# Cross-attention with its loop written out: three PSUM sets, one bank for the sample's heads, outputs written as two parts

## What is computed

```python
def memory_cross_attention(h, mem_k, mem_v, w_q, w_o):     # XA_HEADS = 4, XA_HEAD_DIM = 256, N_MEM = 256
    q = (h @ w_q).reshape(B, L, XA_HEADS, XA_HEAD_DIM)
    s = jnp.einsum('blhd,bmhd->bhlm', q, mem_k).astype(jnp.float32) * (XA_HEAD_DIM ** -0.5)
    p = jax.nn.softmax(s, axis=-1).astype(mem_v.dtype)
    o = jnp.einsum('bhlm,bmhd->blhd', p, mem_v)
    return o.reshape(B, L, D_MODEL) @ w_o
```

## Time and profile before

| | |
|---|---|
| median of 3 runs | 2229.95 us (2228.45 to 2230.43) |
| profiled execution | 2233.87 us, of which the span from the first to the last instruction is 2232.2 us |
| PE busy | 2114.9 us (95%) |
| DVE busy | 1206.9 us (54%) |
| ACT busy | 529.2 us (24%) |
| POOL busy | 189.9 us (9%) |
| mean granted TensorE clock | 0.970 |

### The profile page before, as it was taken

One profiled execution on the slowest core, in us unless ns is written; L12 is line 12 of the kernel. 1 busy time (PEld: TensorE's weight loads), 2 busy tenths in 40 slices (PEclk: granted clock), 3 DMA queues, 4 the chain that ended last, 5 costly groups with the idle time before them and its releaser, 6 DMA issues. The chain is left out here.

```text
span 2232.2 us, 49063 instructions
## 1 busy us (share of the span) xinstructions
PE 2114.9 (95%) x21806; PEld 2009.3 (90%) x21806; DVE 1206.9 (54%) x1695; ACT 529.2 (24%) x971; POOL 189.9 (9%) x255
## 2 busy tenths in 40 slices
PE   8998989998999999996999899998999899999997
PEld 8996769985999999994979899987997799999997
DVE  5435777444655555338549444445663565555433
ACT  2005774013211110002247222225221221101000
POOL 4000001000200000110000322210011010000010
PEclk9998999998999999998999999998999999999998
DMA  4334112460233223231311000004341123222221
GB/s 127 90 111 125 58 29 86 128 184 0 79 88 88 85 85 90 86 89 45 90 57 39 8 4 4 4 13 125 114 161 48 31 85 92 85 85 85 86 86 66
DMA packets 299347, 169.81 MB, mean 76 GB/s; under 512 B 10312, under 2 KB 294160, under 8 KB 299184
## 3 DMA queue, kind: packets, MB, share of 16 engines
q1 hardware_dynamic: 294960, 151.25, 23.5%
q10 hardware_dynamic: 4224, 16.12, 1.9%
HBM read 155.94 MB, written 11.41 MB: 75 GB/s over the span
## 5 line engine op out<-in xcount | busy, mean ns | idle before, releaser
L259 PE MATMUL psum<-words_r,weights_high_r 128*128 128x272 f32 (+1 forms) x7808 | 1498.7, 291 | 16.9 <-DVE words_r L210 13.2
L259 PEld LDWEIGHTS psum<-words_r,weights_high_r 128*128 128x128 f32 x7808 | 1235.9, 190 | 27.2 <-issue 15.0
L259 PE MATMUL psum<-words_r,weight_ring_r 128*128 128x272 f32 (+1 forms) x3904 | 1131.8, 290 | 0.0
L259 PEld LDWEIGHTS psum<-words_r,weight_ring_r 128*128 128x128 f32 x3904 | 739.5, 189 | 0.0
L205 DVE TENSOR_SCALAR weights_high_r<-weight_ring 128x1024 fp32r<-128x1024 f32 (+1 forms) x258 | 176.3, 683 | 522.8 <-PE psum L259 515.3
L210 DVE TENSOR_TENSOR weight_ring_r<-weight_ring,weights_high_r 128x1024 fp32r<-128x1024 f32 (+1 forms) x264 | 319.3, 1209 | 11.2 <-ACT weights_high_r L344 2.4
L399 POOL TENSOR_TENSOR words<-words,words 128x544 f32<-128x544 f32 x42 | 74.5, 1773 | 1283.0 <-ACT words L386 1283.0
L2370 PE MATMUL psum<-words 64*64 64x64 f32 (+1 forms) x3536 | 138.6, 231 | 0.6
L1707 ACT ACTIVATE words<-words 128x544 f32<-128x544 f32 x44 | 29.0, 659 | 454.7 <-DVE words L1650 454.7
L2370 PEld LDWEIGHTS psum<-words 64*64 64x64 f32 x3536 | 129.1, 135 | 3.1 <-DVE words L2293 1.8
L376 DVE TENSOR_TENSOR words<-psum,words 128x544 f32<-128x544 f32 x48 | 34.8, 724 | 129.3 <-PE psum L259 129.3
(11 more groups left out here) (309 smaller groups left out, 1960.2 us busy)
## 6 DMA issues: line engine op xcount, KB each, us to landing
weight_ring<-in_ffn_w_gate_up_dram SPq DMA_DIRECT2D x88, 512.0 KB, 3.8
weight_ring<-in_xa_w_kv_dram SPq DMA_DIRECT2D x32, 512.0 KB, 3.9
weight_ring<-in_ffn_w_down_dram SPq DMA_DIRECT2D x32, 448.0 KB, 3.7
weight_ring<-in_sb_w_qkv_dram SPq DMA_DIRECT2D x24, 512.0 KB, 3.7
weight_ring<-in_xa_w_q_dram SPq DMA_DIRECT2D x16, 512.0 KB, 4.1
weight_ring<-in_xa_w_o_dram SPq DMA_DIRECT2D x16, 512.0 KB, 4.0
weight_ring<-in_ffn_w_down_dram SPq DMA_DIRECT2D x16, 512.0 KB, 4.0
weight_ring<-in_sb_w_o_dram SPq DMA_DIRECT2D x8, 512.0 KB, 4.0
```

What stands on the lines that cost most here:

```text
L259: last = nc.tensor.matmul(c.psum[0:job.m(u), job.bank(q) + h, 0:w], weights[:, k, :], x[:, k, h * w:(h + 1) * w], start=job.opens(u) and k ...
```

## The change

`cross_attention` is written out for four heads, without a loop, copies to fixed buffers or primed semaphores, and POOL has nothing left to do in it. Head g uses PSUM set g % 3 (two banks), so three heads can be open at a time; the fourth waits until the outputs of the first are taken (`o_low`). Banks 6 and 7 belong to the sample. Its four heads lie together in one bank, each in 32 partitions (`lanes`), so that one maximum, one exponential and one scaling serve all; its values are multiplied the other way round (the probabilities are the stationary operand), and the result is transposed back. Maxima are taken over two query tiles at a time. The outputs leave PSUM as halves: ACT writes the high part of a tile, DVE subtracts it and writes the low part; `full` is not written. The order of work on each engine is a written list. In `feed_forward` the `Split` of the attention's outputs is gone, and the column sum of the norm (`norm.tensor`) moves from between units 0 and 1 of `up` into unit 1, after its second tile. The stage makes 23 semaphores instead of 38, the following one 2 fewer. The scratch space changes with it. The ring's weight splits are as before.

```diff
--- before.py
+++ after.py
@@ cross_attention
...
-            with pool.Fori(0, XH // 2) as it:
-                for g, hd in enumerate(heads):
-                    pool.wait_ge(s("scored_s", g), it + PRIMED)
-                    nc.gpsimd.tensor_copy(hd.q, q[:, bass.ds(it * 4 + 2 * g, 2), :]).then_inc(s("q_staged", g), 1)
...
+            def score(g):
+
+                if g >= SETS:
+                    pe.wait_ge(o_low, 2 * (g - SETS) + 2)
+                for i in range(QT):
+                    for kk in range(2):
+                        last = mm(scores(g)[:, i, :], q[:, 2 * g + kk, i * P:(i + 1) * P], kv[:, 2 * g + kk, :],
+                                  start=kk == 0 and i % 2 == 0, stop=kk == 1, skip_group_check=True)
+                    if i % 2:
+                        last.then_inc(scored, 1)
...
+            def score_sample():
+
+                for kk in range(2):
+                    for g, r in enumerate(lanes):
+                        last = mm(c.psum[r, 6, 0:NMEM], q[:, 2 * g + kk, SEQ:T], s_kt[:, 2 * g + kk, :], start=kk == 0, stop=kk == 1,
+                                  skip_group_check=True)
+                last.then_inc(scored_s, 1)
...
+            def weigh(g):
+
+                pe.wait_ge(first_copied, g + 1)
+                pe.wait_ge(second_copied, g + 1)
+                for e in range(2):
                     for m in range(MT):
-                        for i in range(QT):
-                            last = nc.tensor.transpose(hd.wide[m][:, i * P:(i + 1) * P], hd.prob[:, i, m * P:(m + 1) * P], c.ident[:])
...
+                        last = mm(bank(g, e), kv_rows[:, m, D + (2 * g + e) * P:D + (2 * g + e + 1) * P], prob_t[g % SETS][:, m, :],
+                                  start=m == 0, stop=m == MT - 1)
+                    last.then_inc(weighed, 1)
+
+            def weigh_sample():
+
+                pe.wait_ge(copied_s, 1)
+                for m in range(MT):
+                    for g, r in enumerate(lanes):
+                        last = mm(c.psum[r, 7, 0:NMEM], prob_ts[:, m, r], s_v[:, m, 2 * g * P:2 * (g + 1) * P], start=m == 0, stop=m == MT - 1,
+                                  skip_group_check=True)
+                last.then_inc(weighed_s, 1)
...
+            score(0)
+            score(1)
+            score_sample()
+            score(2)
+            turn(0)
+            turn(1)
+            weigh(0)
+            turn_sample()
+            weigh(1)
+            score(3)
+            turn(2)
+            weigh_sample()
+            weigh(2)
+            turn_out_sample()
+            turn(3)
+            weigh(3)
...
+            def take_out(g, e):
+
+                dve.wait_ge(o_high, 2 * g + e + 1)
+                take_low(c, o.low[:, 2 * g + e, 0:SEQ], bank(g, e), o.high[:, 2 * g + e, 0:SEQ]).then_inc(o_low, 1)
+
+            peak(0, 0)
+            peak(0, 1)
+            peak(1, 0)
+            peak(1, 1)
+            scale(0)
+            peak_sample()
+            peak(2, 0)
+            scale(1)
+            peak(2, 1)
+            copy_first(0)
+            copy_first(1)
+            scale_sample()
+            scale(2)
+            take_out(0, 0)
+            take_out(0, 1)
+            take_out(1, 0)
+            take_out(1, 1)
+            peak(3, 0)
+            peak(3, 1)
+            copy_first(2)
+            dve.wait_ge(weighed_s, 1)
+            nc.vector.tensor_copy(rows_s, c.psum[:, 7, 0:NMEM]).then_inc(rows_s_copied, 1)
+            scale(3)
+            take_out(2, 0)
+            take_out(2, 1)
+            for e in range(2):
+                dve.wait_ge(o_s_high, 2)
+                take_low(c, sample_tiles(o.low, e), sample_out(e), sample_tiles(o.high, e)).then_inc(o_s_low, 1)
+            copy_first(3)
+            take_out(3, 0)
+            take_out(3, 1)
...
+            def take_out(g):
+
+                for e in range(2):
+                    act.wait_ge(weighed, 2 * g + e + 1)
+                    nc.scalar.activation(o.high[:, 2 * g + e, 0:SEQ], bank(g, e), ACT.Copy).then_inc(o_high, 1)
+
+            exp(0)
+            exp(1)
+            exp_sample()
+            copy_second(0)
+            copy_second(1)
+            exp(2)
+            take_out(0)
...
+            take_out(1)
+            exp(3)
+            copy_second(2)
+            take_out(2)
...
+            copy_second(3)
+            take_out(3)
@@ feed_forward
+            def sum_norm(k):
+
+                if k == 1:
+                    pe.wait_ge(c.slot_emptied[3], up.emptied[3])
+                    norm.tensor(pe)
+
             for u in range(o.per):
-                multiply_unit(c, pe, o, 0, u, split.low if u == 0 else None)
-            multiply_unit(c, pe, up, 0, 0, norm.low)
-            pe.wait_ge(c.slot_emptied[3], up.emptied[3])
-            norm.tensor(pe)
-            for u in range(1, RING):
+                multiply_unit(c, pe, o, 0, u)
+            for u in range(RING):
                 if u == 3:
                     pe.wait_ge(norm.meaned, 1)
-                multiply_unit(c, pe, up, 0, u)
+                multiply_unit(c, pe, up, 0, u, norm.low if u == 0 else None, sum_norm if u == 1 else None)
...
-            split.scalar(act)
...
             split_unit(c, dve, o, 0, 0)
-            split.vector(dve)
             split_unit(c, dve, o, 0, 1)
```

More of the change, by code:

```diff
@@ L1518, in cross_attention @@
-    heads = [Head(g) for g in range(2)]
-    assert at[0] <= 3 * REGION
-    def s(x, g):
-        return heads[g].sems[x]
+        for w in spaces:
+            if w[2] >= n:
+                ap = c.flat(w[0], n, at=w[1])
+                w[1] += n
+                w[2] -= n
+                return ap if len(shape) == 1 else ap.rearrange("p (a b) -> p a b", a=shape[0])
+        raise AssertionError("no space")
+    prob, prob_t = [part(QT, NMEM) for _ in range(SETS)], [part(MT, SEQ) for _ in range(SETS)]
@@ new lines, in cross_attention @@
+    neg_max, total, inverse = (part(XH, QT) for _ in range(3))
+    prob_s, prob_ts, rows_s = part(NMEM), part(MT, P), part(NMEM)
+    stats_s = part(3)
+    neg_max_s, total_s, inverse_s = (stats_s[:, i:i + 1] for i in range(3))
+    lanes = [slice(g * DEC, (g + 1) * DEC) for g in range(XH)]
+    scored, maxed, exped, inverted, scaled, turned, first_copied, second_copied, weighed, o_high, o_low = (c.sem(f"{name}_{x}") for x in (
+        "scored", "maxed", "exped", "inverted", "scaled", "turned", "first_copied", "second_copied", "weighed", "o_high", "o_low"))
@@ new lines, in score_sample, with turn @@
+            def score_sample():
[4 more added lines that the diff above has]
+                last.then_inc(scored_s, 1)
+            def turn(g):
+                pe.wait_ge(scaled, QT * (g + 1))
+                for m in range(MT):
+                    for i in range(QT):
+                        last = tr(bank(g, m)[:, i * P:(i + 1) * P], prob[g % SETS][:, i, m * P:(m + 1) * P], c.ident[:])
+                    last.then_inc(turned, 1)
@@ L1632, in feed_forward, with exp, exp_sample @@
-def feed_forward(c, name, o, up, down, nxt, split, norm, tail, hidden, gated, out):
+            def exp(g):
+                for i in range(QT):
+                    act.wait_ge(maxed, 2 * g + i // 2 + 1)
+                    nc.scalar.activation(prob[g % SETS][:, i, :], scores(g)[:, i, :], ACT.Exp, bias=neg_max[:, g, i:i + 1],
+                                         accum_out=total[:, g, i:i + 1]).then_inc(exped, 1)
+            def exp_sample():
+                act.wait_ge(maxed_s, 1)
+                nc.scalar.activation(prob_s, c.psum[:, 6, 0:NMEM], ACT.Exp, bias=neg_max_s, accum_out=total_s).then_inc(exped_s, 1)
@@ new lines, in copy_second @@
+            def copy_second(g):
+                act.wait_ge(turned, MT * g + 2)
+                nc.scalar.copy(prob_t[g % SETS][:, 1, :], bank(g, 1)).then_inc(second_copied, 1)
+            def take_out(g):
+                for e in range(2):
+                    act.wait_ge(weighed, 2 * g + e + 1)
[4 more added lines that the diff above has]
+            copy_second(0)
@@ new lines, in _ @@
+            copy_second(1)
+            exp(2)
+            take_out(0)
+            act.wait_ge(turned_s, 1)
+            nc.scalar.copy(prob_ts, c.psum[:, 6, 0:NMEM].rearrange("p (m t) -> p m t", m=MT)).then_inc(copied_s, 1)
+            take_out(1)
+            exp(3)
+            copy_second(2)
+            take_out(2)
+            act.wait_ge(o_s_turned, 1)
+            for e in range(2):
+                nc.scalar.activation(sample_tiles(o.high, e), sample_out(e), ACT.Copy).then_inc(o_s_high, 1)
@@ L1638, in feed_forward @@
+            copy_second(3)
+            take_out(3)
+def feed_forward(c, name, o, up, down, nxt, norm, tail, hidden, gated, out):
     nc = c.nc
```

155 lines of the change are left out of this document (47 added, 108 removed).

## The result

The changed kernel takes 2200.45 us (median of 4 runs, 2196.48 to 2203.73), the kernel before 2230.19 (4 runs). The ratio is 0.9863, with a 95% interval of 0.9842 to 0.9884. That is 29.7 us less by the medians, where 27.1 were forecast (2203). The profiled execution has a span of 2198.3 us.

What follows compares the result with a forecast made beforehand. PE, busy 95% of the span, was taken as the bound. Stages of 44.55 us against 59.96 and 42.05 against 54.99, with 1.16 returning later, gave 27.1 us less: 2203 us, forecast 2199 to 2207, range 2194 to 2214.

Steps and rivals of the forecast that it cites:

- What bounds the stage: Whole kernel: PE is busy 95% of the span, so time is saved where it works slowly or stands still.
- PE's products: Attention stage, higher clock: 33.0 us for four heads, 0.5 small transposes, 2.2 sample, 1.8 waits; 37.5 us in all.
- The sample's products: Sample's scores and weighing: four column groups share the array, 1.1 us each, bounds 0.9 and 3.63; serial rival chance 0.1.
- The change of shape: At the sample's two products: switching to narrow column groups costs about 0.2 us, included in the 1.1 each.
- The waits: PE inside the stage: 0.4 us before weigh(2), 1.4 before weigh(3), all other waits met.
- Entrance and end: PE starts about 0.5 us after the last work before; last product to first of the projection takes 1.5 + 2.55.
- The clock: Layer 0's entrance: a low stretch loses 2.5 us, bounds 0 and 3.3; layer 1's entrance stays at the higher level.
- a fall there: Rival, inside the stage at turn(0), turn(1) and the sample's narrow products: clock falls, up to 3.3 us a layer; chance 0.15.
- the low stretch there stays in both layers, at the same cost: Start of the projection: PE stands still 4.05 us, between 3.5 and 4.7 before, so no difference in clock loss.
- The semaphores: Clearing behind layer 1's attention: the same 1.16 us is paid one stage later, before the outputs are stored; net nothing.
- The size of the whole: Both stretches: 15.4 us less in layer 0, 12.9 in layer 1, 1.16 returning later; together 27.1.
- The halves: Outputs as halves: 1.5 us after the last product, formerly hidden; the next stage's first low part, 0.6 us, goes.

Runs made afterwards that it cites:

- written-out kernel before: The kernel before with its two-pass loop written out and POOL's copies gone, all else as before: 2233.86 us, ratio 1.0003.
- bridge: The changed kernel with 7 small identity matmuls after the last weighing and 9 at the start of the next stage: 2198.89 us, ratio 0.9839.
- early split: The changed kernel with the first weight split inside the attention, and copy_first(3) and turn(3) moved earlier: 2191.11 us; with semaphore clearing limit 80 as well, 2189.49.

## Why the prediction was right, and where it was off

**What bounds the stage**: right in that PE's time is what counts, that POOL's copies were not what held it, and that what the stages gave back reached the end: 32.2 us of stretches, 29.7 of the medians. It looks for the gain where PE stands still or is slow, and the rows bear it out for 19.2 us (11.9 of idle time, 7.3 of the clock). What it leaves out is the largest single item, 11.3 us of the sample's work. The prediction prices the sample's two products only in the new stage (2.2 us) and never beside the old one, where they took 7.2 in each layer. The forecast holds all the same, because it adds up the new stage from nothing and takes the old one as a whole from the windows.

**PE's products**: forecast 37.5 us for the stage with the clock up, measured 1718.52 - 1682.12 = 36.4 in layer 1. The scores were 3.45 to 3.56 and not 3.63. The loop is not the reason: the written-out kernel before has none, and takes the same 1731.59 - 1727.96 = 3.63 for them:

```profile
1727.96 3.70 PE L1538 MATMUL psum<-words,words 128*128 128x256 f32 x16
1731.59 1.05 PE L1542 MATMUL psum<-words,words 128*32 128x256 f32 x4
```

In both, the sample's small products stand at each side of a head's scores. From start to start, instruction by instruction, the trace has 0.30 us between the first two, 0.31 from the last to the sample's first, and 0.216 between all others; the fourth head's scores of the changed kernel, with a weighing before and transposes behind, have 0.216 throughout, 3.45 together. The change gathers the sample's products and so pays these steps less often. The transposes were 0.90 a head and not 1.09, because a duration was taken where a distance was wanted. The two differences, 0.08 in the mean and 0.19, four times, are the 1.1.

**The sample's products**: 1.00 and 1.07 against 1.1. The row of a mixer with two lanes carried the price over to four. The runs show 3.57 in one lane and 1.00 in four. The Trainium skill (TensorEngine Tiling, Theoretical Speedup) gives up to 4x for four tiles side by side; the trace agrees, at 3.6x. The change of shape costs more than the 0.1 by which 1.00 exceeds a quarter of 3.57: from the last full-width product before these 16 instructions to the second one behind them the trace has 1.63 us, where 6 intervals of 0.216 would be 1.30, so 0.33 in all, part of which the rows count to the neighbours; in one lane it is 0.32. The forecast's 0.2 was of this size.

**The waits**: 0.4 and 1.4 forecast, 0.5 and 1.3 measured, and none elsewhere.

**Entrance and end**: 0.5 forecast, 0.46 and 0.32 measured; 1.5 + 2.55 forecast from the last product to the first of the projection, 3.76 measured.

**The clock**: at the entrance of layer 0 I took 2.5 us lost; it was 1.7, as PE was busy for 3.4 in a low stretch half as long. Inside the stages it stayed up; the prediction counted on this, though it lists only one of the three low stretches that the kernel before has there. turn(0) and turn(1), 1.8 us, lie between scores and a weighing, and the clock was at 1.00 through them. The Trainium skill (TensorE: Matmul & The Clock Gate, Part 4) says that transposes in the transpose mode don't count as a busy PE in the same way; by that rule a fall there was likelier. Whether these transposes use that mode the trace doesn't say, and none of the ten profiled executions with three PSUM sets shows a fall at them. Behind the barrier the step "the low stretch there stays in both layers, at the same cost" was mis-sized in layer 1: PE was busy for 6.0 us of it and not 3.2 (busy time of the low stretch from 1757.8 in the trace before), so 1.4 us more were lost behind the stretch; in other kernels with the same code there the low stretch was 3.4 us long. That the pause is the cause is shown by the bridge: with the pause filled, no low stretch follows in either layer.

**The semaphores**: right to 0.1 us.

**The size of the whole**: over both stretches the forecast was 28.3 us and the trace has 32.2. The 3.8 between them are 2.2 of PE's products, 0.8 of the clock and 0.8 of entrances and ends, all to the same side. That the medians still came within 2.6 us of the forecast is in part luck: what was lost behind layer 1's barrier goes the other way, and the spread ahead of the stages is larger than this.

**The halves**: the forecast had them at -0.6 and +0.7, so at nothing; the run that undoes them says +0.6 in each layer, because their low parts also stand ahead of DVE's copy for weigh(3).

## What to carry to other kernels

Price the bound engine's small odd jobs before its pauses: here the sample's work was the largest item. Put small products for several heads in different 32-column groups of the array. Where two units of work in flight leave the bound engine waiting for a chain on others, open a third; but price such parts together, since they fill the same pause (12.6 us together, 20.6 alone). When the stage is dense, look at its end: work of the next stage that needs nothing from this one (here a weight split) belongs in the idle time before the last outputs, and a shorter pause there can also keep the clock up.

## What the runs showed of the hardware

Products in different column groups share the array whether neighbouring instructions alternate between the groups or four of one group stand in a row: 1.00 and 1.02 us for 16 instructions of 256 columns, 3.57 in one group. Going from full-width products to them and back costs about 0.3 us more, in one group or four.

Behind all 22 stage ends with a pause of PE from 3.4 to 4.8 us came a low stretch, 3.4 us long behind ten of them and 6.8 behind twelve; with the same code at the end of the stage and the same pause of 3.8 us both occur (first unit 7.7 to 7.9, or 8.8 to 9.1 us). Behind the four with a pause of 1.8 us (early split) and the two with filler matmuls and 0.3 us between them came none (6.3 to 6.4). The fillers were seven and nine products of the identity with itself.

Up to layer 0's attention the same code took between 489.8 and 497.7 us in those twelve profiled executions: a spread of 8 us ahead of everything that the change touches, beside 7.3 us between the fastest and the slowest whole run of the changed kernel.
